# Moving four activation buffers of a one-core transformer kernel to other places within 256 bytes

## The reference

```python
u = rmsnorm(h, norm_ff_g) @ w_ff1            # 1024 -> 4096
h = h + jnp.square(jax.nn.relu(u)) @ w_ff2   # 4096 -> 1024
a, v = jnp.split(h @ w_up, 2, axis=-1)       # 1024 -> 2 x 2816, twice in the whole
h = h + (silu(causal_dwconv(a)) * v) @ w_down
```

## Time and profile before

| | |
|---|---|
| median of 3 runs | 1066.72 us (1063.89 to 1067.74) |
| the profiled execution | 1063.19 us, of which the span from first to last instruction is 1061.2 us |
| TensorE busy (matmuls) | 1037.6 us, 98% of the span |
| weight loads busy | 985.8 us, 93% |
| VectorE, ScalarE, GpSimd busy | 750.5, 524.0, 146.2 us (71%, 49%, 14%) |
| granted TensorE clock, mean | 0.994 |

### The profile page before, as it was taken

How to read it: one execution, slowest core, us unless ns; L and a number is a source line. 1 busy time by engine, 2 the same in 40 slices (tenths; PEclk the granted TensorE clock), 3 DMA queues, 4 the chain that set the end, 5 groups by cost and what they waited for, 6 DMA issues and landing times. The chain is left out here.

```text
span 1061.2 us, 22387 instructions
## 1 busy us (share of the span) xinstructions
PE 1037.6 (98%) x8509; PEld 985.8 (93%) x8509; DVE 750.5 (71%) x1198; ACT 524.0 (49%) x900; POOL 146.2 (14%) x194
## 2 busy tenths in 40 slices
PE   9999989999999999989999999999999999999998
PEld 8999779999999999858999999999987699999998
DVE  4866878666666666784777677778867677777775
ACT  6453666644444454226644444456645564444442
POOL 0070010011222100002000100040115500100000
PEclk9999999999999999999999999999998999999999
DMA  9553226265555646632565565555730045655561
GB/s 344 159 187 111 60 81 192 89 210 182 182 195 190 188 138 186 182 123 62 182 205 189 183 193 178 185 169 153 237 111 21 1 142 192 190 191 179 187 195 54
DMA packets 51041, 169.71 MB, mean 160 GB/s; under 512 B 5664, under 2 KB 10784, under 8 KB 50848
## 3 DMA queue, kind: packets, MB, share of 16 engines
q1 hardware_dynamic: 45216, 163.22, 47.7%
q10 hardware_dynamic: 5760, 5.57, 2.0%
HBM read 162.15 MB, written 1.05 MB: 154 GB/s over the span
## 5 line engine op out<-in xcount | busy, mean ns | idle before, releaser
L1548 DVE TENSOR_TENSOR WL<-WR,WH 128x1024 fp32r<-128x1024 f32 x302 | 372.8, 1251 | 141.3 <-ACT WH L1281 137.9
L858 PE MATMUL acc<-XH,WH 128*128 128x256 f32 x1360 | 393.2, 289 | 2.2 <-DVE XP L1565 1.7
L860 PE MATMUL acc<-XH,WL 128*128 128x256 f32 x1360 | 384.3, 283 | 0.0
L859 PE MATMUL acc<-XL,WH 128*128 128x256 f32 x1360 | 383.9, 282 | 0.0
L1281 ACT ACTIVATE WH<-WR 128x1024 fp32r<-128x1024 f32 x302 | 312.2, 1050 | 115.5 <-PE acc L860 82.7
L858 PEld LDWEIGHTS acc<-XH,WH 128*128 128x128 f32 x1360 | 259.9, 191 | 6.1 <-DVE WL L1548 3.0
L859 PEld LDWEIGHTS acc<-XL,WH 128*128 128x128 f32 x1360 | 260.0, 191 | 0.9
L860 PEld LDWEIGHTS acc<-XH,WL 128*128 128x128 f32 x1360 | 260.0, 191 | 0.0
L858 PE MATMUL big<-UH,WH 128*128 128x256 f32 x608 | 168.7, 278 | 0.8 <-POOL UL L2068 0.8
L859 PE MATMUL big<-UL,WH 128*128 128x256 f32 x608 | 168.3, 277 | 0.0
L860 PE MATMUL big<-UH,WL 128*128 128x256 f32 x608 | 168.1, 276 | 0.0
(11 more groups left out here) (299 smaller groups left out, 1361.8 us busy)
## 6 DMA issues: line engine op xcount, KB each, us to landing
WR<-weights SPq DMA_DIRECT2D x302, 512.0 KB, 3.6
STK<-UP ACTq DMA_DIRECT2D x32, 138.0 KB, 3.6
X<-x_t SPq DMA_DIRECT2D x4, 256.0 KB, 6.8
MEM<-mem_t SPq DMA_DIRECT2D x1, 1024.0 KB, 10.1
result_t<-X SPq DMA_DIRECT2D x4, 256.0 KB, 2.2
CON<-constants SPq DMA_DIRECT2D x1, 880.0 KB, 11.8
CBUF<-KCV ACTq DMA_DIRECT2D x4, 128.0 KB, 5.3
CBUF<-KCV ACTq DMA_DIRECT2D x4, 127.5 KB, 6.2
```

The lines of the kernel that those rows point to most:

```text
L858: pe.matmul(out, wh, hi, start=start, stop=False, skip_group_check=True)
L859: pe.matmul(out, wh, lo, start=False, stop=False, skip_group_check=True)
L860: return pe.matmul(out, wl, hi, start=False, stop=stop, skip_group_check=True)
L1548: dve.tensor_tensor(WL[:, cs % SPL], WR[:, cs % RAW], WH[:, cs % SPL].bitcast(F32), ALU.subtract).then_inc(w_low, 1)
```

## The change

Three allocations that nothing reads or writes are put between the tensors. 424 floats are 1696 bytes, that is 6 x 256 + 160; 32 floats are 128 bytes; 56 floats are 224 bytes; together 2048 bytes. `XH` and `XL` go from 128 to 32 modulo 256, `YH` and `YL` from 128 to 160, and everything behind them moves by 2048 bytes and keeps its place modulo 256. `X`, `G`, `GY` and `SQ`, ahead of the room, stay. No instruction, wait or transfer is added, taken away or moved.

```diff
         SQ = sb("SQ", [P, KD, T])
+
+        sb("shift", [P, 424])
         XH, XL = sb("XH", [P, KD, T], F32R), sb("XL", [P, KD, T], F32R)
+        sb("shift_y", [P, 32])
         YH, YL = sb("YH", [P, KD, T], F32R), sb("YL", [P, KD, T], F32R)
+        sb("shift_back", [P, 56])
         WR = sb("WR", [P, RAW, CH])
```

## The result

The changed kernel takes 1057.45 us (median of 5 runs, 1056.11 to 1059.06) where the kernel before takes 1067.74 in the same comparison (5 runs, 1063.89 to 1069.78): a ratio of 0.9909, interval 0.9885 to 0.9933. That is 10.3 us faster. The forecast was 1041, so less than half of the 25.5 us came. The time lies near the 1055 of the rival "only unordered".

The account below looks back on a forecast made before the run. The pace at which TensorE starts matmuls was taken as the bound. X's 23.3 and Y's 2.2 us, together 25.5, took the profiled 1063.19 us to 1037.7; the runs' median being 3.5 higher gave 1041 us, range 1028 to 1070.

Parts of the forecast that it names:

- only unordered: Rival for X's matmuls: the new place locks into nothing, X goes at 117.5 ns a start, 1055 us; chance 0.17.
- I take U's pace, since -96 is nearest to U's -64 of the places that the trace has: Step for X's matmuls, 96 bytes below the weights: 113.3 ns a start as U's, saving 23.3 us.
- 120 and 113.3 are both exact over whole tiles, so fixed places do lock: Argument that fixed places give TensorE's starts a steady pace, used against the rival of 117.5 ns and 1055 us.
- U's must stay at 113.3 in any case: Sign in the timeline: U's starts stay 113.3 ns apart, since neither U nor the weights move; otherwise the whole reading falls.
- the reading by relative place: In TensorE, moving-operand read and next weight load hinder each other by relative place: 120 bad, 113 good, 117 to 118 unordered.
- Y was sized right: Term for Y's matmuls, 32 bytes above the weights: half of what U's pace would give, 2.2 us saved.
- No cost elsewhere: Token-major parts, `compress` and writers of moved buffers were taken as nothing; the supply of weights was said to have room.
- The place is not what counts: Rival: the moving operand's place does not set TensorE's pace, so nothing changes, 1066.7 us; chance 0.13.
- Off the grid: slower: Rival: places off multiples of 64 bytes slow X to 122 to 126.7 ns a start, 1077 to 1095 us; chance 0.22.
- The forecast's mechanism: Moving X and Y off the weights' place modulo 256 speeds TensorE's matmul starts; 25.5 us saved in all, chance 0.48.
- the prediction's figure for X: Sum for X's tiles in the feed-forwards and elsewhere: 3.8, 11.9 and 7.6, together 23.3 us saved.

## Why the prediction was wrong

- **The failed step is "I take U's pace, since -96 is nearest to U's -64 of the places that the trace has".** X at 96 below goes at 117.3 in the first feed-forward and 117.99 on the whole. With 117.5 for 113.3 the prediction's own sum is that of its rival, 9.4 + 2 us: 1055 against 1057.45. That it comes so near is partly luck: in the trace X gained 6.2 us, its longer gaps counted, and U lost 2.1, which the rival's sum doesn't have. Nearness in bytes carried nothing: 0 gave 120.0, -64 gave 113.3 or 117.8, -96 gave 117 to 119, -128 gave 118.8. Even U's own place did not promise U's pace: X at 64 brought 11.7 us.
- **The argument against that rival failed too.** "120 and 113.3 are both exact over whole tiles, so fixed places do lock" holds for settled starts (X's first nine behind U are not at 120), and X's new place does lock in the first feed-forward: into a cycle of five distances whose mean is 117.4. What I read as unordered is an order of its own. The chance of 0.17 for this case was far too low, since only two locks were known and a third could lie anywhere between.
- **"U's must stay at 113.3 in any case" was wrong**, and so was the conclusion tied to it. U went at 2.82 us a tile in the second gated stage and lost 2.1 us over the trace, yet the reading by relative place holds: moving the weights, with U kept at its distance from them, took 5.3 and 4.3 ns a start from X and Y, which stayed where they were, and moving U alone cost it 5.9. What I had left out is that a place has more than one pattern. That the work before selects it is likely, not shown.
- **Y was sized right, by luck**: 2.2 us forecast, 2.1 measured (120.44 to 117.61 ns). The forecast put 32 above halfway between the bad place and 113.3 at a distance of 64; but 64 above gave 117.8 and not 113.3, so the far end of that estimate does not exist.
- **No cost elsewhere, as forecast.** `WL` did not become a wait of TensorE, and the instruction counts of all engines are the same. With the weights at 192, where TensorE is faster still, its waits begin with the same 2.6 us.
- **"The place is not what counts"** is refuted by moved addresses. The same matmuls went 120.0 ns apart with U at the weights' place and 113.3 with U 64 below it. The page SBUF — State Buffer of the Trainium skill, section Who interferes with whom, gives the moving operand and the weight load independent read ports; by that their relative place would not count, and the runs show that it does.
- **"Off the grid: slower"** is refuted: X's settled starts are 117.4 ns apart and not over 121, and Y at 160 was faster than at 128.
- **The forecast's mechanism paid where its place was used**: with every moving operand 64 below the weights, the kernel takes 1039.6 us, close to the 1041 that the prediction had for 96 below. The gain comes from what it counted: X's starts went from 119.75 to 114.08 ns, over some 4110 of them, without longer gaps, 23.3 us, which is the prediction's figure for X. Y's went from 120.44 to 115.72, but in that profiled execution Y had 76 gaps over 200 ns, where before had 32, and they took that gain back.

## What to carry to other kernels

Where TensorE is full and its starts lie a few per cent over the shortest that the trace shows, compare the place modulo 256 of the moving operand with that of the stationary one: with 256 float32r columns and a weight load for each matmul, equal places cost 120.0 ns a start here, 64 bytes below cost 113.3 or, in some stages, 117.8. Moving the weights, and U with them, did better here than moving X and Y, for a reason that stays open. Measure the very place that you mean to use, and don't interpolate between places. Read the distance stage by stage, since a place can hold more than one steady pattern, and take several runs of a kernel whose time spreads.

## What the runs showed of the hardware that was not expected

- The pace by relative place, from the feed-forwards: 0: 120.0 ns; 64 below: 113.3 or 117.8; 96 below: 117.3, or 118.1 where 5.63 and 5.70 us a step take turns; 128 off: about 118.8; 64 above: 117.8. Below all of them is a weight load alone, 112.
- The patterns are steady and go on through tiles and across changes of the PSUM tile. In the second gated feed-forward of the changed kernel U goes at 117.7 behind X's 118.1; in the first, at 113.7 behind X's 117.3, with the same addresses.
- A room of 64 bytes ahead of the weights and one ahead of `UH` changed the time of an otherwise equal program by 2.5%, and one ahead of `UH` alone took it the other way in its one run.
